# Reordering the opening of the input projection in a hybrid-decoder kernel on one Trainium2 core

## The chip, the cores and the metric

The kernel runs on one core of one Trainium2 chip. The metric is the device time of one execution in microseconds (us); the median of three runs is compared. Five engines are named as in the profile: PE (TensorE: matmuls and transposes; PEld is its weight load), ACT (ScalarE), DVE (VectorE), POOL (GpSimd) and SP (SyncE, which here only issues transfers). Each runs its own list of instructions in order and waits for the others by semaphores. PE and PEld read SBUF and write PSUM, whose eight banks hold 128 x 512 floats each.

## The reference, cut to what matters

One decoder layer over 2048 tokens of 1024 channels. Only its first step is touched:

```python
z = rms_norm(h, norm_attn_g[i]) @ w_in[i]     # (2048, 1024) @ (1024, 2304)
# rms_norm: x * rsqrt(mean(x*x) + 1e-6) * g
```

The columns of z are queries, keys and values of eight attention heads, the inputs of a spatial gate, and 256 channels of a state-space layer. Attention adds a bias to its scores, looked up from rel_bias (32 buckets x 8 heads) by distance; the kernel makes all the bias lines it needs once, inside the same stage.

## The kernel before

The whole kernel is a sequence of stages (input projection, attention, state space, mixing, feed-forward, final part). Each stage ends with a barrier over all engines. The change is in the first stage, `project_in`, which takes the time from 0 to about 460 us.

**Tiling.** The tokens go in G = 4 groups of 512 (four tiles of 128 rows, TILES = 4), the columns of `w_in` in NBLK = 9 blocks of 256, the 1024 input channels in KC = 8 chunks of 128. Each operand is split into a high part and the remainder, and each product is three matmuls per chunk (high by high, high by low, low by high), accumulated over the eight chunks. The order is written out by hand: for each group, all nine column blocks.

**What happens for a group before its products.** ACT squares the four row tiles with a running sum (`square`, L1044); DVE adds epsilon (L1102); ACT takes the root (`root`, L1049); DVE inverts it (L1104) and multiplies each of the four row tiles by it in place (`scale_rows`, L1107). PE transposes the scaled rows, one chunk of channels (four 128 x 128 transposes) a time, into one PSUM bank (`turn`, L1139). ACT writes the high part of that bank to SBUF, scaled by the gain (`split_x`, L1053), DVE the remainder (its own `split_x`, L1111). The turns alternate between two banks (`turn_bank`), so turn k waits until the remainder of turn k - 2 is written.

**Weights.** SP loads a block of weights (`load_w`, L970, 1 MB); ACT writes its high part (`split_w`, L1059), POOL the remainder (L1186). Two weight buffers alternate, so the load of block B + 2 waits for POOL's remainder of block B.

**PSUM.** Four banks (`product_bank`) take the products in turn, two (`turn_bank`) the transposes, two (`spare_bank`) are spare. The three matmuls of the bias look-up (L1165, one for each attention branch, 33 x 8 by 33 x 384) use the two spare banks and the last product bank; DVE copies them out (L1121).

**Order at the start.** SP issues four row tiles (L966), weight block 0, the look-up table (L1007), after a wait for a DVE memset the bias rows (L1009), weight block 1, seven small parameter loads, and then waits for the three bias copies before it goes on to the main loop. ACT: four squares, `split_w(0)`, `root(0)`, eight `split_x`, then the main loop, which begins with `split_w(1)`. DVE: memset, `scale_rows(0)`, eight `split_x`, three bias copies, a spreading copy of a parameter (L755), then group 1. PE: eight turns, the look-up, a wait for all eight remainders and for the three bias copies, and then the products of the main loop, each block behind its `w_lo_ready`. The lines of PE's opening:

```python
for k in range(KC):
    turn(0, k)
pe.wait_ge(bias_loaded, 2 * DMA)
for b in range(NB):
    pe.matmul(bias_bank[b][0:NH, 0:BAND], per_head[:, :], lookup[:, b, :], start=True, stop=True).then_inc(looked_up, 1)
pe.wait_ge(lo_written, KC)
pe.wait_ge(bias_copied, NB)
```

Of the kernel before, what the change touches and what calls it, by code (L numbers as in the profile page):

```python
# [22 lines left out]
P = 128  # L23
# [285 lines left out]
BAND = 384  # L309
# [571 lines left out]
def project_in(nc, x, gain, w_in, qk_hi, qk_lo, z, u_channels, rel_bias, bias_table, bias_lines, bands, bands_stored, parameters, head_ahead, ident):  # L881
# [27 lines left out]
    with Stage(nc, "in") as st:  # L909
# [30 lines left out]
        block = st.block()  # L940
        parameters.allocate(st, spare_bank[0], rows.rearrange("p t d -> p (t d)"), squares[:, 0, 0:2 * P], spare[:, 0:2 * P])
        assert nc.sbuf_base <= SSM_AT, nc.sbuf_base
        bias_bank = [spare_bank[0], spare_bank[1], product_bank[RING - 1]]

        def blocks():
            for g in range(G):
# [16 lines left out]
        def _(sp):  # L963
# [39 lines left out]
                    sp.dma_start(dst, src).then_inc(head_ahead.loaded, DMA)  # L1003

            load_x(0)
            load_w(0)
            sp.dma_start(lookup[:, :, :], bias_table).then_inc(bias_loaded, DMA)  # L1007
            sp.wait_ge(ones_set, 1)
            sp.dma_start(per_head[0:BUCKETS, :], rel_bias).then_inc(bias_loaded, DMA)  # L1009
            load_w(1)  # L1010
            parameters.load(sp)
            sp.wait_ge(bias_copied, NB)
# [24 lines left out]
        @block.scalar  # L1037
        def _(act):
            def square(g, t):
                n = g * TILES + t  # L1040
                act.wait_ge(x_loaded[t], (g + 1) * DMA)
                if n >= 2:
                    act.wait_ge(mean_ready, n - 1)
                nc.scalar.activation(squares[:, n % 2], rows[:, t], ACT.Square, scale=D ** -0.5,  # L1044
                                     accum_out=mean_sq[:, g, t:t + 1]).then_inc(mean_ready, 1)

            def root(g):
                act.wait_ge(eps_added, g + 1)
                nc.scalar.activation(rms[:, g], mean_sq[:, g], ACT.Sqrt).then_inc(rms_ready, 1)  # L1049

            def split_x(g, k):
                act.wait_ge(transposed, g * KC + k + 1)
                nc.scalar.activation(hi[:, g % 2, k, :], turn_bank[k % 2][:, :], ACT.Identity, scale=g_cols[:, k:k + 1]).then_inc(hi_written, 1)  # L1053

            def split_w(B):
                act.wait_ge(w_loaded[B % 2], (B // 2 + 1) * DMA)
                if B >= 2:
                    act.wait_ge(product_ready, units_to[B - 1])
                nc.scalar.copy(w_hi[B % 2][:, :, :], w_raw[B % 2][:, :, :]).then_inc(w_hi_ready, 1)  # L1059

            def evict(u):
                r = u % RING
                width = BANK if is_qk[u] else WIDE
                if u >= RING:
                    act.wait_ge(stored[r], stores_through(u - RING))
                act.wait_ge(product_ready, u + 1)
                if is_qk[u]:
                    nc.scalar.copy(result_hi[:, r, :], product_bank[r][:, :]).then_inc(result_hi_ready, 1)
                if is_u[u]:
                    nc.scalar.copy(result[:, r, :].rearrange("p (l m) -> p l m", l=L),  # L1070
                                   product_bank[r].rearrange("p (m l) -> p l m", l=L)).then_inc(copied, 1)
                else:
                    nc.scalar.copy(result[:, r, 0:width], product_bank[r][:, 0:width]).then_inc(copied, 1)

            for t in range(TILES):
                square(0, t)
            split_w(0)
            root(0)
            act.wait_ge(gain_loaded, DMA)
            for k in range(KC):  # L1080
                split_x(0, k)
            for g, b, B in blocks():
                if B + 1 < G * NBLK:
                    split_w(B + 1)
                if g + 1 < G:
                    if 1 <= b <= TILES:
                        square(g + 1, b - 1)
                    if b == TILES:
                        root(g + 1)
                    if b > LOOK:  # L1090
                        for k in (2 * (b - LOOK - 1), 2 * (b - LOOK - 1) + 1):
                            split_x(g + 1, k)
                if B == (G - 1) * NBLK + LOOK + 1:
                    parameters.root(act)
                for u in units_of(B):
                    evict(u)

        @block.vector
        def _(dve):
            def scale_rows(g):  # L1100
                dve.wait_ge(mean_ready, (g + 1) * TILES)
                nc.vector.tensor_scalar(mean_sq[:, g], mean_sq[:, g], EPS, None, ALU.add).then_inc(eps_added, 1)  # L1102
                dve.wait_ge(rms_ready, g + 1)
                nc.vector.reciprocal(rstd[:, g], rms[:, g]).then_inc(rstd_ready, 1)  # L1104
                dve.wait_ge(rstd_ready, g + 1)
                for t in range(TILES):
                    nc.vector.tensor_scalar(rows[:, t], rows[:, t], rstd[:, g, t:t + 1], None, ALU.mult).then_inc(rows_scaled, 1)  # L1107

            def split_x(g, k):
                dve.wait_ge(hi_written, g * KC + k + 1)  # L1110
                nc.vector.scalar_tensor_tensor(lo[:, g % 2, k, :], turn_bank[k % 2][:, :], g_cols[:, k:k + 1],  # L1111
                                               hi[:, g % 2, k, :].bitcast(F32), ALU.mult, ALU.subtract).then_inc(lo_written, 1)

            nc.vector.memset(per_head[:, :], 1.0).then_inc(ones_set, 1)
            scale_rows(0)
            dve.wait_ge(gain_loaded, DMA)
            for k in range(KC):
                split_x(0, k)
            for b in range(NB):
                dve.wait_ge(looked_up, b + 1)  # L1120
                nc.vector.tensor_copy(bias_rows[:, b, :], bias_bank[b][0:NH, 0:BAND]).then_inc(bias_copied, 1)  # L1121
            parameters.spread_dt(dve)
            for g in range(1, G):
                scale_rows(g)
# [8 lines left out]
        def _(pe):  # L1133
            def turn(g, k):
                pe.wait_ge(rows_scaled, (g + 1) * TILES)
                if g * KC + k >= 2:
                    pe.wait_ge(lo_written, g * KC + k - 1)
                for t in range(TILES):
                    mm = pe.transpose(turn_bank[k % 2][:, t * P:(t + 1) * P], rows[:, t, k * P:(k + 1) * P], ident[:, :])  # L1139
                mm.then_inc(transposed, 1)  # L1140

            def product(u, g, B, n):
# [5 lines left out]
                        pe.wait_ge(result_hi_ready, qk_to[u - RING] + 1)  # L1148
                part = slice(n * P, (n + 1) * P)
                for k in range(KC):  # L1150
                    if is_qk[u] or is_u[u]:
                        pe.matmul(out[:, :], w_hi[w][:, k, part], x_hi[:, k, :], start=(k == 0), stop=False)
                        pe.matmul(out[:, :], w_hi[w][:, k, part], x_lo[:, k, :], start=False, stop=False)
# [4 lines left out]
                        mm = pe.matmul(out[:, 0:WIDE], x_lo[:, k, part], w_hi[w][:, k, :], start=False, stop=(k == KC - 1))  # L1158
                mm.then_inc(product_ready, 1)

            for k in range(KC):
                turn(0, k)
            pe.wait_ge(bias_loaded, 2 * DMA)
            for b in range(NB):
                pe.matmul(bias_bank[b][0:NH, 0:BAND], per_head[:, :], lookup[:, b, :], start=True, stop=True).then_inc(looked_up, 1)  # L1165
            pe.wait_ge(lo_written, KC)
            pe.wait_ge(bias_copied, NB)
            for g, b, B in blocks():
                if b == 0:
                    pe.wait_ge(lo_written, (g + 1) * KC)  # L1170
                if g + 1 < G and b > LOOK:
                    for k in (2 * (b - LOOK - 1), 2 * (b - LOOK - 1) + 1):
# [2116 lines left out]
```

## Time and profile before

| | us |
|---|---|
| runs, median (lowest to highest of three) | 2695.56 (2693.56 to 2697.71) |
| the profiled execution, its own time | 2699.88 |
| span of its trace | 2698.3 |
| mean granted clock of PE over the span | 0.975 |
| PE busy over the span | 2529.6 |

The span runs from the first to the last instruction of the trace; the execution's own time holds 1.58 us more around it. All times in the views are counted from the start of the span. The duration of a matmul in the trace is modelled at its end, and successive matmuls overlap, so a row that merges several gives start and total length, and their pace is read from the distance of starts.

### The profile page before, as it was taken

The page shows a single profiled execution, that of the slowest core. Times are in us where ns is not written, and L with a number is a line of the kernel's source. Part 1 is how long each engine was busy: PE and PEld are TensorE (multiplying, and loading weights), DVE is VectorE, ACT ScalarE, POOL GpSimd, SP SyncE. Part 2 cuts the span into 40 slices and gives each one's busy share as a digit, 9 for nine tenths or more (in the row PEclk, how much of TensorE's full clock was granted, in tenths as well). Part 3 has the DMA queues.
Part 4 walks back from the last instruction along what each step waited for, and adds up shares of the span by engine and source line. Part 5 has one row for each costly group of instructions (what it writes and reads, how often), then busy time and mean ns, then how long its engine had stood idle before and what let it go on. Part 6 is the DMA issues. An engine that isn't in the chain of part 4 may idle for free. (4 is left out here: it accounts for less than half of the span.)

```text
span 2698.3 us, 38124 instructions
## 1 busy us (share of the span) xinstructions
PE 2529.6 (94%) x13395; PEld 2169.2 (80%) x13395; DVE 1805.3 (67%) x3343; ACT 1347.5 (50%) x2425; POOL 825.7 (31%) x625
## 2 busy tenths in 40 slices
PE   6999999999976899699999989999999999999998
PEld 4989888999965688588888868888888877887876
DVE  2113276777766777689999976768898885563433
ACT  3343432666644666555555545545555554344544
POOL 2554544656620221235565540001222221000000
PEclk9999999999987899899999999999999999999999
DMA  4675564788853355134444477543232336763211
GB/s 160 200 221 172 164 178 144 179 180 186 174 154 122 105 168 200 56 122 148 163 154 157 153 270 265 188 164 99 100 114 98 106 133 222 285 224 110 81 70 49
DMA packets 317450, 420.97 MB, mean 156 GB/s; under 512 B 31073, under 2 KB 229025, under 8 KB 312522
## 3 DMA queue, kind: packets, MB, share of 16 engines
q1 hardware_dynamic: 292090, 332.68, 40.9%
q0 software_dynamic: 25184, 86.01, 8.6%
q8 instruction: 102, 1.67, 0.3%
q14 instruction: 74, 0.61, 0.1%
HBM read 298.59 MB, written 124.16 MB: 157 GB/s over the span
## 5 line engine op out<-in xcount | busy, mean ns | idle before, releaser
L2783 PE MATMUL ffn_bank<-ffn_x,ffn_ring 128*128 128x512 f32 x704 | 275.9, 392 | 15.3 <-DVE ffn_strips L2583 9.2
L2784 PE MATMUL ffn_bank<-ffn_x,ffn_ring 128*128 128x512 f32 x704 | 274.8, 390 | 0.0
L2785 PE MATMUL ffn_bank<-ffn_x,ffn_ring 128*128 128x512 f32 x704 | 274.7, 390 | 0.0
L2851 POOL DMA_DIRECT2D ffn_act<-ffn_late x154 | 85.6, 557 | 474.5 <-DVE ffn_late L2615 444.4
L1186 POOL TENSOR_TENSOR in_w_lo<-in_w,in_w_hi 128x2048 fp32r<-128x2048 f32 x36 | 168.1, 4670 | 191.2 <-ACT in_w_hi L1059 191.2
L2783 PE MATMUL ffn_bank<-tail_shared,ffn_ring 128*128 128x512 f32 x528 | 206.7, 392 | 9.3 <-DVE ffn_ring L2558 7.8
L629 ACT ACTIVATE att_exps<-att_scores,att_part 128x256 f32<-128x256 f32 (+1 forms) x384 | 152.9, 454 | 107.4 <-DVE att_part L597 104.9
L2785 PE MATMUL ffn_bank<-tail_shared,ffn_ring 128*128 128x512 f32 x528 | 206.4, 391 | 0.0
L2380 ACT COPY ffn_strips<-ffn_bank 128x512 f32<-128x512 f32 x176 | 103.5, 588 | 144.1 <-PE ffn_bank L2785 144.1
L2599 DVE SCALAR_TENSOR_TENSOR ffn_strips<-ffn_strips,ffn_taps 128x512 f32<-128x512 f32 x176 | 143.9, 818 | 41.1 <-ACT ffn_strips L2395 41.1
L2783 PEld LDWEIGHTS ffn_bank<-ffn_x,ffn_ring 128*128 128x128 f32 x704 | 132.6, 188 | 46.0 <-issue 11.5
L567 PE MATMUL att_bank<-att_v,att_expsT 128*128 128x66 f32 x1200 | 154.2, 270 | 5.3 <-DMA att_v<-z_rows 4.0
L2566 DVE TENSOR_TENSOR ffn_ring<-ffn_w,ffn_ring 128x2048 fp32r<-128x2048 f32 (+1 forms) x42 | 91.1, 2169 | 98.2 <-ACT ffn_ring L2354 98.2
L2785 PEld LDWEIGHTS ffn_bank<-ffn_x,ffn_ring 128*128 128x128 f32 x704 | 132.7, 188 | 28.0
L2784 PEld LDWEIGHTS ffn_bank<-ffn_x,ffn_ring 128*128 128x128 f32 x704 | 132.7, 189 | 27.3
L567 PEld LDWEIGHTS att_bank<-att_v,att_expsT 128*128 128x128 f32 x1200 | 147.7, 193 | 7.0 <-issue 4.2
L2602 DVE SCALAR_TENSOR_TENSOR ffn_strips<-ffn_strips,ffn_taps 128x512 f32<-128x512 f32 x176 | 141.8, 806 | 6.2
L1156 PE MATMUL in_bank<-in_w_hi,in_hi 128*128 128x256 f32 x512 | 145.8, 285 | 0.0
L1157 PE MATMUL in_bank<-in_w_lo,in_hi 128*128 128x256 f32 x512 | 144.8, 283 | 0.0
L1158 PE MATMUL in_bank<-in_w_hi,in_lo 128*128 128x256 f32 x512 | 144.8, 283 | 0.0
L2345 ACT CAST ffn_ring<-ffn_sums 128x512 fp32r<-128x512 f32 x176 | 107.9, 614 | 62.7 <-PE ffn_bank L2785 52.2
L2784 PE MATMUL ffn_bank<-ffn_x_lo,ffn_ring 128*128 128x512 f32 x352 | 137.0, 389 | 0.0
(437 smaller groups left out, 7375.8 us busy)
## 6 DMA issues: line engine op xcount, KB each, us to landing
ffn_w<-in_ffn_w_up SPq DMA_DIRECT2D x88, 512.0 KB, 4.8
ffn_act<-ffn_late POOLq DMA_DIRECT2D x154, 256.0 KB, 2.3
in_w<-in_w_in SPq DMA_DIRECT2D x36, 1024.0 KB, 6.5
ffn_a_raw<-ffn_act SPq DMA_DIRECT2D x77, 256.0 KB, 3.7
ffn_a_raw_later<-ffn_act SPq DMA_DIRECT2D x77, 256.0 KB, 4.5
ffn_w<-ffn_down_sums SPq DMA_DIRECT2D x16, 1024.0 KB, 5.2
ffn_w<-in_ffn_w_down SPq DMA_DIRECT2D x12, 1024.0 KB, 5.7
ffn_pieces<-in_ffn_w_down POOLq DMA_DIRECT2D x44, 256.0 KB, 3.5
```

The costliest lines, as they stand in the source:

```text
L567: mm = pe.matmul(out, expsT[:, n % 2, piece * P:(piece + 1) * P], vals[:, b, blk, h * ROW:(h + 1) * ROW], start=(at == 0), stop=(at == len ...
L629: nc.scalar.activation(exps[:, n % RING, m * width:(m + 1) * width], scores[:, n % RING, m * width:(m + 1) * width], ACT.Exp, bias=part[:, ...
L1156: pe.matmul(out[:, 0:WIDE], x_hi[:, k, part], w_hi[w][:, k, :], start=(k == 0), stop=False)
L1157: pe.matmul(out[:, 0:WIDE], x_hi[:, k, part], w_lo[w][:, k, :], start=False, stop=False)
L1158: mm = pe.matmul(out[:, 0:WIDE], x_lo[:, k, part], w_hi[w][:, k, :], start=False, stop=(k == KC - 1))
L1186: nc.gpsimd.tensor_tensor(w_lo[B % 2][:, :, :], w_raw[B % 2][:, :, :], w_hi[B % 2][:, :, :].bitcast(F32), ALU.subtract).then_inc(w_lo_read ...
L2345: nc.scalar.copy(slot(j)[0], src).then_inc(w_hi_ready, 1)
L2599: nc.vector.scalar_tensor_tensor(conv[:, n, tg], raw[f % 2][:, n, 1 + tg * BANK:1 + (tg + 1) * BANK], tap[1], conv[:, n, tg], ALU.mult, AL ...
L2602: nc.vector.scalar_tensor_tensor(conv[:, n, tg], raw[f % 2][:, n, tg * BANK:(tg + 1) * BANK], tap[0], conv[:, n, tg], ALU.mult, ALU.add).t ...
L2783: pe.matmul(out[:, :], hi[:, k], x_hi[kind][:, k], start=(k == 0 and fresh), stop=False, skip_group_check=not fresh)
L2784: pe.matmul(out[:, :], hi[:, k], x_lo[kind][:, k], start=False, stop=False, skip_group_check=not fresh)
L2785: mm = pe.matmul(out[:, :], lo[:, k], x_hi[kind][:, k], start=False, stop=(k == KH - 1), skip_group_check=not fresh)
```

## The change

It is confined to the opening of `project_in`, group 0. PE does the bias look-up first and the eight turns after it. The eight turns of group 0 go to eight different banks (`first_turns`: product banks 0 to 2, the two turn banks, then the three banks of the look-up, whose order is changed so that the last product bank comes first), so none waits for a remainder any more; the last three wait for the bias copies of their bank. PE's wait for all eight remainders before the first products is replaced by one wait for each chunk inside the first product (unit u = 0). ACT takes the root ahead of `split_w(0)`, and scales two of the four row tiles of group 0 itself (a new function, `scale_first_rows`); DVE scales the other two, and makes the bias copies ahead of its eight remainders. SP issues the look-up table and the bias rows ahead of weight block 0. Groups 1 to 3 and everything after are as before.

```diff
@@ -940,7 +940,9 @@
         block = st.block()
         parameters.allocate(st, spare_bank[0], rows.rearrange("p t d -> p (t d)"), squares[:, 0, 0:2 * P], spare[:, 0:2 * P])
         assert nc.sbuf_base <= SSM_AT, nc.sbuf_base
-        bias_bank = [spare_bank[0], spare_bank[1], product_bank[RING - 1]]
+        bias_bank = [product_bank[RING - 1], spare_bank[0], spare_bank[1]]
+        first_turns = product_bank[0:RING - 1] + turn_bank + bias_bank
+        SCALED_BY_DVE = TILES // 2
 
         def blocks():
             for g in range(G):
@@ -1003,10 +1005,10 @@
                     sp.dma_start(dst, src).then_inc(head_ahead.loaded, DMA)
 
             load_x(0)
-            load_w(0)
             sp.dma_start(lookup[:, :, :], bias_table).then_inc(bias_loaded, DMA)
             sp.wait_ge(ones_set, 1)
             sp.dma_start(per_head[0:BUCKETS, :], rel_bias).then_inc(bias_loaded, DMA)
+            load_w(0)
             load_w(1)
             parameters.load(sp)
             sp.wait_ge(bias_copied, NB)
@@ -1048,9 +1050,15 @@
                 act.wait_ge(eps_added, g + 1)
                 nc.scalar.activation(rms[:, g], mean_sq[:, g], ACT.Sqrt).then_inc(rms_ready, 1)
 
+            def scale_first_rows():
+                act.wait_ge(rstd_ready, 1)
+                for t in range(SCALED_BY_DVE, TILES):
+                    nc.scalar.activation(rows[:, t], rows[:, t], ACT.Copy, scale=rstd[:, 0, t:t + 1]).then_inc(rows_scaled, 1)
+
             def split_x(g, k):
                 act.wait_ge(transposed, g * KC + k + 1)
-                nc.scalar.activation(hi[:, g % 2, k, :], turn_bank[k % 2][:, :], ACT.Identity, scale=g_cols[:, k:k + 1]).then_inc(hi_written, 1)
+                src = turn_bank[k % 2] if g else first_turns[k]
+                nc.scalar.activation(hi[:, g % 2, k, :], src[:, :], ACT.Identity, scale=g_cols[:, k:k + 1]).then_inc(hi_written, 1)
 
             def split_w(B):
                 act.wait_ge(w_loaded[B % 2], (B // 2 + 1) * DMA)
@@ -1074,8 +1082,9 @@
 
             for t in range(TILES):
                 square(0, t)
+            root(0)
+            scale_first_rows()
             split_w(0)
-            root(0)
             act.wait_ge(gain_loaded, DMA)
             for k in range(KC):
                 split_x(0, k)
@@ -1103,22 +1112,23 @@
                 dve.wait_ge(rms_ready, g + 1)
                 nc.vector.reciprocal(rstd[:, g], rms[:, g]).then_inc(rstd_ready, 1)
                 dve.wait_ge(rstd_ready, g + 1)
-                for t in range(TILES):
+                for t in range(TILES if g else SCALED_BY_DVE):
                     nc.vector.tensor_scalar(rows[:, t], rows[:, t], rstd[:, g, t:t + 1], None, ALU.mult).then_inc(rows_scaled, 1)
 
             def split_x(g, k):
                 dve.wait_ge(hi_written, g * KC + k + 1)
-                nc.vector.scalar_tensor_tensor(lo[:, g % 2, k, :], turn_bank[k % 2][:, :], g_cols[:, k:k + 1],
+                src = turn_bank[k % 2] if g else first_turns[k]
+                nc.vector.scalar_tensor_tensor(lo[:, g % 2, k, :], src[:, :], g_cols[:, k:k + 1],
                                                hi[:, g % 2, k, :].bitcast(F32), ALU.mult, ALU.subtract).then_inc(lo_written, 1)
 
             nc.vector.memset(per_head[:, :], 1.0).then_inc(ones_set, 1)
             scale_rows(0)
+            for b in range(NB):
+                dve.wait_ge(looked_up, b + 1)
+                nc.vector.tensor_copy(bias_rows[:, b, :], bias_bank[b][0:NH, 0:BAND]).then_inc(bias_copied, 1)
             dve.wait_ge(gain_loaded, DMA)
             for k in range(KC):
                 split_x(0, k)
-            for b in range(NB):
-                dve.wait_ge(looked_up, b + 1)
-                nc.vector.tensor_copy(bias_rows[:, b, :], bias_bank[b][0:NH, 0:BAND]).then_inc(bias_copied, 1)
             parameters.spread_dt(dve)
             for g in range(1, G):
                 scale_rows(g)
@@ -1133,10 +1143,13 @@
         def _(pe):
             def turn(g, k):
                 pe.wait_ge(rows_scaled, (g + 1) * TILES)
-                if g * KC + k >= 2:
+                if g:
                     pe.wait_ge(lo_written, g * KC + k - 1)
+                elif first_turns[k] in bias_bank:
+                    pe.wait_ge(bias_copied, bias_bank.index(first_turns[k]) + 1)
+                out = turn_bank[k % 2] if g else first_turns[k]
                 for t in range(TILES):
-                    mm = pe.transpose(turn_bank[k % 2][:, t * P:(t + 1) * P], rows[:, t, k * P:(k + 1) * P], ident[:, :])
+                    mm = pe.transpose(out[:, t * P:(t + 1) * P], rows[:, t, k * P:(k + 1) * P], ident[:, :])
                 mm.then_inc(transposed, 1)
 
             def product(u, g, B, n):
@@ -1148,6 +1161,8 @@
                         pe.wait_ge(result_hi_ready, qk_to[u - RING] + 1)
                 part = slice(n * P, (n + 1) * P)
                 for k in range(KC):
+                    if u == 0:
+                        pe.wait_ge(lo_written, k + 1)
                     if is_qk[u] or is_u[u]:
                         pe.matmul(out[:, :], w_hi[w][:, k, part], x_hi[:, k, :], start=(k == 0), stop=False)
                         pe.matmul(out[:, :], w_hi[w][:, k, part], x_lo[:, k, :], start=False, stop=False)
@@ -1158,15 +1173,13 @@
                         mm = pe.matmul(out[:, 0:WIDE], x_lo[:, k, part], w_hi[w][:, k, :], start=False, stop=(k == KC - 1))
                 mm.then_inc(product_ready, 1)
 
-            for k in range(KC):
-                turn(0, k)
             pe.wait_ge(bias_loaded, 2 * DMA)
             for b in range(NB):
                 pe.matmul(bias_bank[b][0:NH, 0:BAND], per_head[:, :], lookup[:, b, :], start=True, stop=True).then_inc(looked_up, 1)
-            pe.wait_ge(lo_written, KC)
-            pe.wait_ge(bias_copied, NB)
+            for k in range(KC):
+                turn(0, k)
             for g, b, B in blocks():
-                if b == 0:
+                if b == 0 and g:
                     pe.wait_ge(lo_written, (g + 1) * KC)
                 if g + 1 < G and b > LOOK:
                     for k in (2 * (b - LOOK - 1), 2 * (b - LOOK - 1) + 1):
```

## Rows read from the trace of the kernel before

**Rows 1.** Page: span, and busy time of each engine.

```profile
span 2698.3 us, 38124 instructions
...
PE 2529.6 (94%) x13395; PEld 2169.2 (80%) x13395; DVE 1805.3 (67%) x3343; ACT 1347.5 (50%) x2425; POOL 825.7 (31%) x625
```

**Rows 2.** Windows: stretch and length, then busy time and count of each engine, clock, DMA.

```profile
0.00:38.40 38.40, 11.72 (x38) 6.62 (x38) 13.31 (x19) 16.55 (x21) 8.21 (x9) 1.00 0.37 117
38.40:100.00 61.60, 60.14 (x266) 49.78 (x267) 10.23 (x7) 21.69 (x32) 31.71 (x13) 1.00 0.65 210
```

**Rows 3.** Waits of PE, whole span: who waited for whom, total, times, longest.

```profile
PE in_bank L1139 <- DVE in_rows L1107: 27.2, 4, 23.5
...
PE in_bank L1152 <- POOL in_w_lo L1186: 4.4, 1, 4.4
```

**Rows 4.** Timeline, 0 to 23.5 us: start, length, engine, line, operation, idle before.

```profile
2.56 1.28 ACT L1044 ACT_TABLE_LOAD   x1 [2.56 <-PEq L139]
...
6.21 1.06 ACT L1044 ACTIVATE in_squares<-in_rows 128x1024 f32<-128x1024 f32 x1 [2.37 <-DMA in_rows<-in_x]
...
12.13 0.19 ACT L1044 ACTIVATION_READ_ACCUMULATOR in_squares<-in_rows 128x1 f32 x1
...
14.44 1.90 ACT L1059 CAST in_w_hi<-in_w 128x2048 fp32r<-128x2048 f32 x1 [2.13 <-DMA in_w<-in_w_in]
16.36 1.28 ACT L1049 ACT_TABLE_LOAD   x1
16.42 4.49 POOL L1186 TENSOR_TENSOR in_w_lo<-in_w,in_w_hi 128x2048 fp32r<-128x2048 f32 x1 [12.24 <-ACT in_w_hi L1059]
17.65 0.21 ACT L1049 ACTIVATE in_rms<-in_mean_sq 128x4 f32<-128x4 f32 x1
...
18.10 5.35 DVE L1107 TENSOR_SCALAR in_rows<-in_rows,in_rstd 128x1024 f32<-128x1024 f32 x4
```

**Rows 5.** Line L1107 over the span: shortest, median and longest duration in ns.

```profile
L1107 DVE TENSOR_SCALAR in_rows<-in_rows,in_rstd x16: 740/748/3364, 18.1 to 307.4; 128x1024 f32<-128x1024 f32 x16
```

**Rows 6.** Transfers in two stretches: 0 to 10 us, and 12.5 to 14.5 us.

```profile
DMA packets 593, 2.05 MB, mean 205 GB/s; under 512 B 85, under 2 KB 96, under 8 KB 593
...
DMA packets 551, 0.61 MB, mean 303 GB/s; under 512 B 75, under 2 KB 518, under 8 KB 551
```

**Rows 7.** Timeline, 23.5 to 38.8 us, from the first turn to the first products.

```profile
23.51 1.97 PE L1139 MATMUL in_bank<-whole_ident,in_rows 128*128 128x128 f32 x8 [23.51 <-DVE in_rows L1107]
24.72 1.48 ACT L1053 ACTIVATE in_hi<-in_bank,in_gain 128x512 fp32r<-128x512 f32 x2 [6.86 <-PE in_bank L1139]
...
31.01 1.60 DVE L1111 SCALAR_TENSOR_TENSOR in_lo<-in_bank,in_gain,in_hi 128x512 fp32r<-128x512 f32 x2 [1.14 <-ACT in_hi L1053]
...
31.91 1.94 PE L1139 MATMUL in_bank<-whole_ident,in_rows 128*128 128x128 f32 x8 [0.80 <-DVE in_lo L1111]
...
33.78 4.00 PE L1165 MATMUL in_bank<-in_lookup,in_per_head 33*8 33x384 f32 x6
...
37.82 0.55 DVE L1121 COPY in_bias_rows<-in_bank 8x384 f32<-8x384 f32 x1 [0.73 <-PE in_bank L1165]
...
38.47 0.76 PE L1152 MATMUL in_bank<-in_hi,in_w_hi 128*128 128x512 f32 x1 [0.69 <-issue]
...
38.74 0.40 SPq L970 DMA_DIRECT2D in_w<-in_w_in  x1
```

**Rows 8.** Windows around the first products, columns as in rows 2.

```profile
38.45:43.30 4.85, 4.83 (x12) 3.79 (x13) 2.59 (x1) 0.00 (x0) 2.51 (x1) 1.00 0.72 220
43.30:52.10 8.80, 8.80 (x40) 7.27 (x39) 0.00 (x0) 0.65 (x2) 0.00 (x0) 1.00 0.75 272
```

**Rows 9.** Line L1139 at groups 1 to 3: durations in ns.

```profile
L1139 PE MATMUL in_bank<-whole_ident,in_rows x88: 272/273/331, 109.4 to 346.1; 128*128 128x128 f32 x88
```

**Rows 10.** Waits of ACT, 40 to 460 us, columns as in rows 3.

```profile
ACT in_w_hi L1059 <- DMA in_w<-in_w_in: 29.9, 11, 6.6
```

**Rows 11.** Windows of two later stretches, columns as in rows 2.

```profile
870.00:900.00 30.00, 18.07 (x72) 14.54 (x72) 24.58 (x48) 21.31 (x32) 6.54 (x6) 0.73 0.10 37
...
960.00:990.00 30.00, 30.00 (x152) 25.33 (x152) 23.60 (x59) 20.01 (x40) 5.92 (x9) 1.00 0.56 169
```

## The prediction, made before the changed kernel ran

> **What bounds the kernel now.** I read the page first. PE is busy 94% of the span [rows 1], so a change can gain only where PE stands still, or where it works slower than it could. The windows then say where that is at the start: in the first 38.4 us PE works 11.7 us, and from there to 100 us it works 60.1 of 61.6 us [rows 2]. The waits of PE say what the standstill is made of: one wait of 23.5 us for the scaled rows of group 0, the longest single wait of PE that this change touches [rows 3]. So the opening is a chain of latencies that ends when the first product starts at 38.47 [rows 7]; after it PE runs almost without a gap. What the change is worth is how much earlier that product starts, less what comes back later.
>
> The timeline gives the chain. The four squares end at 12.32. ACT then goes into the weight split, which waits for its weights until 14.44 and takes 1.90; only then come the table load of 1.28, the root at 17.65, and the scaling by DVE from 18.10 to 23.45 [rows 4]. Those four scalings last 5.35 together, although the median of one is 0.748; one of the sixteen in the kernel lasted 3.364 [rows 5]. It is the first: POOL's remainder of the weights runs from 16.42 to 20.91 [rows 4], and three of 0.66 each before 23.45 put its end at 21.46, just after POOL's. So 2.7 us of the scaling is DVE held while POOL works. Then the turns: two banks let PE do two, then it waits; the first pair starts at 23.51 and the fourth at 31.91, 2.80 a pair, of which 1.87 is PE's work (31.91 to 33.78). The look-up takes 4.0, its last copy ends at 38.37, and the product follows [rows 7].
>
> **The change part by part.** Times are on the clock of this trace.
>
> *Root ahead of the weight split.* The table load follows the last square at 12.33. A load need not stand behind what its activation waits for: the first one ran at 2.56, 3.65 us ahead of the square that waited for its rows [rows 4]. Load 12.33 to 13.62; root to 13.83; from the root's start to the first scaling the trace has 0.45 (17.65 to 18.10), so scaling starts at 14.08 instead of 18.10.
>
> *Scaling by two engines.* DVE: two tiles, 0.66 and 0.75, end 15.5, with POOL idle until then, since its work comes behind the weight split that ACT now does later. ACT: the form with a factor for each row is not in the trace at this size; the nearest row is the square of the same tile, 1.06 [rows 4]. Two give 2.1, so ACT ends at 16.2. Below it cannot be under 1.9 (the cast of 2048 columns, 1.90); above, 2.3: by 1.06 for 1024 columns and 1.90 for 2048, 512 would take 0.64, and the evacuation of 512 with a factor takes 0.74 [rows 7], so a factor may add 0.1 to each tile. Rows are ready at 16.2 instead of 23.5.
>
> *Look-up first.* It costs PE 4.0 at the head of its queue, behind the landing of the two bias transfers; behind it stand all turns. The rows of x are 2.1 MB, and 2.05 MB had moved by 10.0 [rows 6]; the table (148.5 KB) now follows them directly, so I take 11.9 for its landing. The fourth row tile was being squared by 11.1 to 11.2 (1.06 a square, its sum read at 12.13 [rows 4]), and nothing behind it lands earlier; the transfers of under 512 B between 12.5 and 14.5, 75 of them [rows 6], hold the tail of both weight block 0 and the bias rows, so 14.5 is the other end. Look-up 11.9 to 15.9: hidden under the scaling, with 0.3 to spare. Landing at 14.5 would put the first turn at 18.5 and so cost 2.3. The three copies on DVE (0.55 each) run from 15.9 to 17.6; turn 5, the first that needs one, comes at about 20.7.
>
> *Weight block 0 behind the table.* SP issues it later, but its packets wait behind x anyway. It lands later by the time of 148.5 KB, about 0.5 us at the pace of the first 10 us, at 15.0 instead of 14.44. ACT comes to it at 16.2: hidden.
>
> *ACT and POOL.* Weight split 16.2 to 18.1; POOL's remainder starts 0.06 to 0.08 later and takes 4.5 [rows 4]: ready at 22.7. Then ACT writes eight high parts at 0.74 each, 18.1 to 24.0. DVE's remainders at 0.80 each (1.60 for two) follow to 25.3 [rows 7].
>
> *Eight banks.* The turns run without a stop. Four pairs at 1.87 are 7.5; that counts the handover to another kind of matmul four times instead of once, so I take 7.2 (6.1 would be the least, if the 0.42 by which the last transpose overhangs a pair is taken off each). Turns 16.2 to 23.4.
>
> *Wait for each chunk.* The first product needs the remainder of chunk 0 (19.6), POOL's 22.7, and PE free at 23.4. Chunk k is ready at 19.6 + 0.8k and wanted at 23.4 + 1.2k (twelve matmuls, four chunks, took 4.85 [rows 8]). No wait. First product: 23.4, set by PE's turns, with POOL 0.7 behind.
>
> *Behind it.* Block 1 is wanted 13.6 us after the first product (38.47 to about 52.1), at 37.0. ACT splits its weights 24.0 to 25.9, POOL is done at 30.5. SP's next loads wait for POOL (22.7) and the last turn (23.4): weight block 2, issued at 38.74, or 0.27 after the first product [rows 7], goes out about 0.7 before it. The spreading copy on DVE comes at 25.3. None is late. Each later stage starts behind a barrier, so it only moves.
>
> **Sum.** 38.47 less 23.4 is 15.1 us. The profiled execution, 2699.88, would become 2684.8; it stood 4.3 above the median of its runs, 2695.56, so the median becomes 2680.5, or 0.56% less. About 0.2% (5.4 us) is what a measurement of this kernel can tell from no change.
>
> **The rivals.**
>
> *The clock rises before the products.* The first twelve matmuls took 0.40 each, the next forty 0.22 [rows 8]: the first stretch is 1.2 GHz by its pace, the second 2.4, although the granted clock reads 1.00 in both. Now PE would have 11.5 us of work without a real gap before the product, where it had stops of 0.9 in each pair. If the clock rose in there, a transpose would last 273 ns [rows 9] for the 0.42 here, the turns would end by 21, POOL (22.7) would start the products, and the twelve would take 2.7 instead of 4.85. That is 15.8 + 2.1 = 17.9, or 2677.7. Against it: in the old order PE worked from 31.91 to 37.8 without a stop, transposes and look-up, and the twelve were still slow. The Trainium skill ("TensorE: Matmul & The Clock Gate", section "Part 4: PE-mode transpose") says that transposes do not count as PE being busy for the clock; by it this rival falls, and the opening here agrees as far as it goes.
>
> *The bias lands late.* PE stands before the look-up until 14.5: 18.5 + 7.2 = 25.7, a gain of 12.8, or 2682.8. For it: the small transfers in the window to 14.5. Against: these lay behind a megabyte of weights that is no longer in front.
>
> *No change: the gain is given back in the stream of weights.* ACT waited eleven times for weights, 29.9 in all [rows 10], and PE 4.4 once for what follows from it [rows 3]. If loads were bound to something that doesn't move, PE would meet them earlier; 9.7 us of new standstill would bring the time within 0.2% (2690 to 2695.6). Against: every load waits for a POOL or PE step that moves too.
>
> *Slower: a later stretch falls to the lower clock.* At 870 to 900 us the granted clock was 0.73, with PE busy 18.1 of 30; at 960 to 990 it was 1.00, with PE busy throughout [rows 11]. Work of PE done anew at half the clock costs its own length again, so from 20.5 us of such work on the kernel is slower by over 0.2% (above 2701). Against: the clock follows PE's own pauses there, which come from chains that only move in time.
>
> **How the numbers follow.** Chances: my forecast 0.74, clock early 0.12, bias late 0.08, gain given back 0.04, slower 0.02. So faster 0.94, same 0.04, slower 0.02. The time is that of the forecast, 2680.5. The range takes in the two cases next to it (2677.7 and 2682.8) and the spread of a median of runs that differ by 2 us to either side (2693.56 to 2697.71 before), with one more for the bounds of ACT's scaling and the turns: 2675 to 2687.
>
> **What would show it.** In the new profile: table load at 12.3, root at 13.6, first scaling at 14.1 with no DVE scaling over 0.8 us; look-up from 11.9 to 15.9; 32 transposes in one run from 16.2 to 23.4; POOL's first remainder ready at 22.7; first product at 23.4, its first twelve matmuls at 0.40; standstill of PE from 38.4 on no larger than before. The forecast is wrong if the table load waits, if ACT's scaling takes over 1.3 a tile, if the look-up starts after 12.5, or if PE's waits behind 40 us grow by more than 5.

## The result, and the profile after

The changed kernel takes 2677.57 us (median of four runs, 2675.45 to 2681.47) against 2695.72 for the kernel before beside it: ratio 0.9939, 95% interval 0.9926 to 0.9951, or 18.2 us less. The forecast was 15.1 less (2680.5), the range 2675 to 2687. Run once more beside other kernels it gave 2680.45 against 2698.45, ratio 0.9930 (0.9915 to 0.9944). The gain is real and larger than forecast by about 3 us; it is very near the rival to which the prediction gave 0.12, that PE's clock rises before the products (2677.7).

The page and the windows of the changed kernel, answering to [rows 1, 2, 8]; the third window has the length of the first of [rows 8] (in a window: length, then busy time and count of PE, PEld, DVE, ACT and POOL, PE's granted clock, busy share of the DMA engines, GB/s):

```profile
span 2677.4 us, 38120 instructions
...
PE 2528.1 (94%) x13395; PEld 2169.1 (81%) x13395; DVE 1797.1 (67%) x3341; ACT 1349.0 (50%) x2427; POOL 824.7 (31%) x625
...
0.00:23.08 23.08, 10.17 (x38) 6.56 (x38) 7.07 (x14) 15.62 (x21) 6.32 (x8) 1.00 0.65 196
23.08:84.68 61.60, 60.16 (x286) 50.44 (x287) 9.82 (x11) 26.74 (x37) 34.70 (x14) 1.00 0.68 221
...
23.08:27.93 4.85, 4.83 (x21) 4.03 (x22) 1.82 (x4) 2.55 (x3) 2.22 (x1) 1.00 0.77 243
```

The stretch before the first product is 15.3 us shorter, with the same instructions of PE in it (38, by [rows 2] too). The 61.6 us behind it hold 286 matmuls where they held 266, with the same busy time: PE does not only start earlier, it works faster at the start. The 4.85 us that held 12 matmuls hold 21.

The timeline of the opening, answering to [rows 4, 7] (the three matmuls of the look-up stand as six in the trace):

```profile
12.46 4.00 PE L1178 MATMUL in_bank<-in_lookup,in_per_head 33*8 33x384 f32 x6 [12.46 <-DMA in_per_head<-in_rel_bias]
12.47 0.19 ACT L1046 ACTIVATION_READ_ACCUMULATOR in_squares<-in_rows 128x1 f32 x1
...
12.67 1.28 ACT L1051 ACT_TABLE_LOAD   x1
...
13.97 0.21 ACT L1051 ACTIVATE in_rms<-in_mean_sq 128x4 f32<-128x4 f32 x1
...
14.42 2.19 ACT L1056 ACTIVATE in_rows<-in_rows,in_rstd 128x1024 f32<-128x1024 f32 x2 [0.25 <-DVE in_rstd L1113]
14.42 1.42 DVE L1116 TENSOR_SCALAR in_rows<-in_rows,in_rstd 128x1024 f32<-128x1024 f32 x2
...
16.52 1.88 ACT L1067 CAST in_w_hi<-in_w 128x2048 fp32r<-128x2048 f32 x1
16.66 6.17 PE L1152 MATMUL in_bank<-whole_ident,in_rows 128*128 128x128 f32 x32 [0.20 <-ACT in_rows L1056]
...
18.48 4.56 POOL L1199 TENSOR_TENSOR in_w_lo<-in_w,in_w_hi 128x2048 fp32r<-128x2048 f32 x1 [14.30 <-ACT in_w_hi L1067]
19.10 5.68 DVE L1121 SCALAR_TENSOR_TENSOR in_lo<-in_bank,in_gain,in_hi 128x512 fp32r<-128x512 f32 x8 [1.88 <-ACT in_hi L1061]
...
23.10 0.50 PE L1167 MATMUL in_bank<-in_hi,in_w_hi 128*128 128x512 f32 x1 [0.27 <-POOL in_w_lo L1199]
23.43 0.40 PE L1168 MATMUL in_bank<-in_lo,in_w_hi 128*128 128x512 f32 x1
23.67 0.39 PE L1169 MATMUL in_bank<-in_hi,in_w_lo 128*128 128x512 f32 x1
```

The table load stands right behind the last square, both engines scale at once, the 32 transposes go in one run, and the first product waits 0.27 for POOL. The second and third product are 0.24 apart, where the first twelve of the old opening are 0.43 apart: the clock is up already. The durations of the transposes show where it rose (line L1152 in 20.5 to 21, 21.5 to 22 and 22 to 23 us; shortest, median, longest in ns), to be held against the 273 ns of [rows 9]:

```profile
L1152 PE MATMUL in_bank<-whole_ident,in_rows x5: 421/421/421, 20.1 to 21.0; 128*128 128x128 f32 x5
...
L1152 PE MATMUL in_bank<-whole_ident,in_rows x5: 272/334/421, 21.2 to 21.9; 128*128 128x128 f32 x5
...
L1152 PE MATMUL in_bank<-whole_ident,in_rows x8: 272/272/273, 21.8 to 22.6; 128*128 128x128 f32 x8
```

So it rose between 21.4 and 21.8, inside the turns: the first transpose at the short duration starts 5.1 us behind the first of them. PE's waits, answering to [rows 3]:

```profile
PE in_bank L1178 <- DMA in_per_head<-in_rel_bias: 12.5, 1, 12.5
...
PE in_bank L1167 <- POOL in_w_lo L1199: 4.7, 2, 4.5
PE in_bank L1152 <- DVE in_rows L1116: 3.7, 3, 1.4
```

The 23.5 us of standstill are 12.5. What was left over for groups 1 to 3 (3.7) and for the weights (4.4, now 4.7 with the 0.27 above) is as before. By the line views the last products of the stage begin at 447.8 instead of 465.8 and attention at 450.0 instead of 468.0: 18.0 us, of which 15.4 are the earlier first product and 2.3 the faster first dozen (the thirteenth matmul starts at 25.95 instead of 43.64); the remaining 0.3 comes behind the long wait for weights, which ends 17.7 earlier (388.22 and 405.92).

### The profile page after: what moved, and what is told of

It is laid out like the page before. It is cut to its first block and busy times, and to the rows that moved or that the text cites. A ratio compares the mean times of both kernels' runs of the same rounds, so it can differ in the third digit from the quotient of the medians.

```text
span 2677.4 us, 38120 instructions
## 1 busy us (share of the span) xinstructions
PE 2528.1 (94%) x13395; PEld 2169.1 (81%) x13395; DVE 1797.1 (67%) x3341; ACT 1349.0 (50%) x2427; POOL 824.7 (31%) x625
```

## The experiments

Theory A: a run of transposes without a stop raises PE's clock; the old opening had the same transposes with a stop in every pair. Rivals: B, it is PE's whole work from the look-up on; C, transposes count for nothing and the look-up did it. The other experiments price the parts. Since the landing of x varies from run to run (the last square's sum was read between 11.7 and 12.6), starts of the first product are also given from the ready rows.

**Root alone, in the old order** (`root_alone`).

```diff
-            split_w(0)
             root(0)
+            split_w(0)
             act.wait_ge(gain_loaded, DMA)
```

> The kernel before with one line moved: the root ahead of the weight split. If the chain of the prediction holds, DVE starts scaling at about 14.1, its fourth tile starts at 16.1, ahead of POOL's remainder at 16.4, so the rows are ready at 16.8 instead of 23.5 and the first product starts at 31.8 instead of 38.5: 6.7 us gained, ratio 0.9975. Rival: DVE's last tile comes a little late, POOL is first and holds it until about 21: rows ready at 21.5, 2 us gained, ratio 0.9993. In both the first twelve products stay at 0.40 each, since the turns stop after each pair as before.

Measured: 2691.65 against 2697.24, ratio 0.9981 (0.9971 to 0.9990). The timeline:

```profile
13.68 2.74 DVE L1107 TENSOR_SCALAR in_rows<-in_rows,in_rstd 128x1024 f32<-128x1024 f32 x4
...
16.14 4.67 POOL L1186 TENSOR_TENSOR in_w_lo<-in_w,in_w_hi 128x2048 fp32r<-128x2048 f32 x1 [11.97 <-ACT in_w_hi L1059]
16.48 1.97 PE L1139 MATMUL in_bank<-whole_ident,in_rows 128*128 128x128 f32 x8 [16.48 <-DVE in_rows L1107]
...
31.44 0.77 PE L1152 MATMUL in_bank<-in_hi,in_w_hi 128*128 128x512 f32 x1 [0.68 <-issue]
```

Four tiles take 2.74 on DVE instead of 5.35, as the last of them has begun before POOL starts, and the first product starts 7.0 us earlier (31.44 against 38.47). One moved line gives 7.0 of the 15.4 in the trace; the medians differ by 5.6. The first nine products are slow (0.43 apart), where it was twelve.

**Look-up behind the turns** (`lookup_behind`): the turns have nothing ahead of them.

```diff
-            pe.wait_ge(bias_loaded, 2 * DMA)
-            for b in range(NB):
-                pe.matmul(bias_bank[b][0:NH, 0:BAND], per_head[:, :], lookup[:, b, :], start=True, stop=True).then_inc(looked_up, 1)
             for k in range(KC):
                 turn(0, k)
+            pe.wait_ge(lo_written, KC)
+            pe.wait_ge(bias_loaded, 2 * DMA)
+            for b in range(NB):
+                pe.matmul(bias_bank[b][0:NH, 0:BAND], per_head[:, :], lookup[:, b, :], start=True, stop=True).then_inc(looked_up, 1)
```

(DVE's copies go behind its remainders, and the wait for them to the product that reuses the bank; the waits inside the first product go.)

> The changed kernel with the look-up behind the eight turns (and behind all remainders) instead of ahead of them. Theory A: a run of transposes without a stop raises PE's clock by itself. Then the pace of the turns rises about 4.9 us behind the first turn, near 21.5, as in the changed kernel (16.66 and 21.5). Theory B: it is PE's whole run from the look-up on, or the look-up itself, that raised it. Then all 32 transposes stay at 421 ns. In both, PE stands from the last turn to the last remainder (about 2 us), the look-up costs 2 to 4 us in front of the products, so the first product starts at 27 to 29.5: 4 to 8 us slower than the changed kernel, ratio to before 0.9955 to 0.997.

Measured: 2683.38, ratio 0.9953 (0.9940 to 0.9967). PE's timeline, and two windows:

```profile
16.50 5.51 PE L1150 MATMUL in_bank<-whole_ident,in_rows 128*128 128x128 f32 x32 [16.50 <-ACT in_rows L1056]
...
24.38 2.10 PE L1179 MATMUL in_bank<-in_lookup,in_per_head 33*8 33x384 f32 x6 [2.36 <-DVE in_lo L1121]
...
27.30:30.60 3.30, 3.30 (x9) 2.59 (x8) 2.39 (x1) 0.00 (x0) 2.31 (x1) 0.52 0.66 164
30.60:33.00 2.40, 2.40 (x12) 1.97 (x11) 0.00 (x0) 0.00 (x0) 0.00 (x0) 1.00 1.08 396
```

The transposes alone raise the clock: 32 in 5.51, the first at the short duration 3.8 us behind the first of all (4.9 was expected), and the look-up then takes 2.10 instead of 4.00. B and C fall. The first product starts at 26.41, ahead of the expected 27 to 29.5. And the clock came down again, at 27, behind a stop of 2.36 and the look-up, with a granted clock of 0.52 until 30.6. So the look-up did not keep the clock up.

**Turns in two banks** (`two_banks`): the same turns with stops.

```diff
-        first_turns = product_bank[0:RING - 1] + turn_bank + bias_bank
+        first_turns = turn_bank * (KC // 2)
...
-                elif first_turns[k] in bias_bank:
-                    pe.wait_ge(bias_copied, bias_bank.index(first_turns[k]) + 1)
+                elif k >= 2:
+                    pe.wait_ge(lo_written, k - 1)
```

(The wait for the bias copies goes to the product that reuses their bank.)

> The changed kernel with the first eight turns in the two turn banks, each waiting for the remainder two turns back; all else as changed. The four pairs then take 2.8 us each: first turn at 16.6, first product at 27.0 instead of 23.1. Theory A (only turns without a stop raise the clock): no rise in the turns, the first twelve products at 0.40 each, so 3.9 + 2.1 = 6 us less gain, about 12 of 18, ratio 0.9955. Theory B (PE's work from the look-up on, stops or none): the rise comes at about 21.5 all the same, and the products start fast: 3.9 us less gain, ratio 0.9947.

Measured: 2685.31, ratio 0.9960 (0.9947 to 0.9974). The first product starts 10.4 us behind the first turn (26.40 and 15.99) instead of 6.4 (23.10 and 16.66). PE's timeline from the last pair of turns to the first products:

```profile
24.81 1.94 PE L1152 MATMUL in_bank<-whole_ident,in_rows 128*128 128x128 f32 x8 [0.80 <-DVE in_lo L1121]
26.40 0.78 PE L1169 MATMUL in_bank<-in_hi,in_w_hi 128*128 128x512 f32 x1
...
26.98 0.63 PE L1170 MATMUL in_bank<-in_lo,in_w_hi 128*128 128x512 f32 x1
...
27.40 0.56 PE L1171 MATMUL in_bank<-in_hi,in_w_lo 128*128 128x512 f32 x1
...
27.80 0.40 PE L1169 MATMUL in_bank<-in_hi,in_w_hi 128*128 128x512 f32 x1
```

The transposes with stops between them did not raise the clock in 10 us. The products were slow at first, as A has it, but three of them, not twelve. The last pair of turns runs into them without a stop, so here a stretch of work without a stop begins at 24.81, and the first fast product starts 3.0 us behind that. In the old opening and in `root_alone`, where a stop of 0.7 stands ahead of the products, the first fast one starts 5.2 and 3.9 behind the first product.

**Extra transposes ahead** (`turns_ahead`).

```diff
+            for n in range(44):
+                pe.transpose(product_bank[0][:, n % TILES * P:(n % TILES + 1) * P], ident[:, :], ident[:, :])
             pe.wait_ge(bias_loaded, 2 * DMA)
```

> The changed kernel with 44 extra transposes of the identity at the head of PE's queue, into a bank that the first turn overwrites; nothing reads them. Theory A: the clock rises inside them, 4 to 6 us behind their start near 3 us, the look-up takes about 2 us instead of 4.0, and the 32 turns come at full clock (273 ns, 4.3 us instead of 6.2). The first product then waits for POOL alone, at 23.0: time as for the changed kernel, within 0.5 us. Theory C (transposes do not count for the clock): the extra ones last 421 ns to their end, the look-up 4.0, and the turns rise no earlier than about 21.5.

Measured: 2680.44, ratio 0.9942 (0.9928 to 0.9955). PE's timeline:

```profile
2.60 6.31 PE L1177 MATMUL in_bank<-whole_ident 128*128 128x128 f32 x44 [2.60 <-PEq L139]
12.49 4.01 PE L1180 MATMUL in_bank<-in_lookup,in_per_head 33*8 33x384 f32 x6 [3.57 <-DMA in_per_head<-in_rel_bias]
16.77 6.43 PE L1152 MATMUL in_bank<-whole_ident,in_rows 128*128 128x128 f32 x32 [0.27 <-ACT in_rows L1056]
```

Half right. The clock rose inside the extra transposes: at the slow pace, 0.21 apart, 44 would take about 9.6 us (an estimate), and they took 6.3. But I had overlooked the stop until the bias landed: behind 3.57 us of it the look-up was slow (4.01) and the turns began slow again. The first product started at 23.20, near the expected 23.0, but not by the way expected.

**Prices of the other parts**, each undone by itself.

`weights_ahead`:

```diff
             load_x(0)
+            load_w(0)
             sp.dma_start(lookup[:, :, :], bias_table).then_inc(bias_loaded, DMA)
...
-            load_w(0)
             load_w(1)
```

> The changed kernel with weight block 0 issued ahead of the look-up table and the bias rows again. By the chain (look-up at PE's head, turns behind it) the bias lands between 13.5 and 14.5 instead of 12.46, the look-up ends at 17.5 to 18.5 instead of 16.46, and turns and first product come 1 to 2 us later (first product 24 to 25 instead of 23.1). Rival: the landing of the bias is set by what lies ahead of both, and it stays at 12.5: no difference.

`all_remainders`:

```diff
-                        pe.wait_ge(lo_written, k + 1)
+                        pe.wait_ge(lo_written, KC)
```

> The changed kernel with the first product waiting for all eight remainders instead of one for each chunk. The last remainder ended at 24.8 in the changed kernel, so the first product starts at 24.8 to 24.9 instead of 23.1: 1.7 us later. PE stands 2 us between turns and products. If the clock that the turns raised outlasts that stop, the products go at 0.23 each from the start; if not, the first ten or so take 0.43 and the loss is 1.7 + 2 = 3.7.

`root_behind`:

```diff
+            split_w(0)
             root(0)
             scale_first_rows()
-            split_w(0)
```

> The changed kernel with root and scaling behind the weight split again. Weights land at about 15, split to 16.9, table load and root to 18.4, scaling from 18.7. Theory: POOL's remainder (17.0 to 21.5) holds DVE's first tile until it ends, so a tile of DVE lasts over 3 us while ACT's two are done at 20.9; rows ready at 22.8, first turn 22.9, first product at 29.2, 6.1 later. Rival: POOL does not hold DVE, both engines scale at once: rows ready at 20.9, first product at 27.2, 4.1 later.

`scaled_by_dve`:

```diff
-        SCALED_BY_DVE = TILES // 2
+        SCALED_BY_DVE = TILES
```

> The changed kernel with all four tiles of group 0 scaled by DVE. DVE takes 14.4 to 17.2, ACT splits the weights from their landing at 15 on, POOL starts at 17.0, behind the start of DVE's last tile (16.4). Rows ready at 17.2 instead of 16.6, first product 0.4 to 0.6 later, and POOL 1.5 earlier than before it is needed. Rival: POOL comes ahead of DVE's last tile and holds it until 21.5, first product 5 later.

Measured, beside 2700.03 for the kernel before: 2683.18, ratio 0.9937 (0.9919 to 0.9954); 2684.20, 0.9944 (0.9927 to 0.9961); 2689.41, 0.9959 (0.9945 to 0.9973); 2678.34, 0.9924 (0.9908 to 0.9941). By their times only the third stands apart from the changed kernel (0.9930, 0.9915 to 0.9944), and barely: its interval overlaps that of the changed kernel's first measurement (0.9926 to 0.9951). All four are read from the timelines. `weights_ahead`, then `all_remainders`:

```profile
15.59 4.00 PE L1178 MATMUL in_bank<-in_lookup,in_per_head 33*8 33x384 f32 x6 [15.59 <-DMA in_per_head<-in_rel_bias]
...
24.84 0.48 PE L1167 MATMUL in_bank<-in_hi,in_w_hi 128*128 128x512 f32 x1
```

```profile
24.40 0.47 PE L1167 MATMUL in_bank<-in_hi,in_w_hi 128*128 128x512 f32 x1 [2.51 <-DVE in_lo L1121]
24.71 0.40 PE L1168 MATMUL in_bank<-in_lo,in_w_hi 128*128 128x512 f32 x1
```

Behind 1 MB of weights the bias lands at 15.59, not at 14.5 as I had bounded it, and the first product is 1.7 later than in the changed kernel. Waiting for all remainders costs 1.3 (1.5 from the table load, which stood 0.23 earlier here), and the clock outlasts a stop of 2.51: the second product follows 0.31 behind the first. `root_behind`, then `scaled_by_dve`:

```profile
16.95 4.51 POOL L1199 TENSOR_TENSOR in_w_lo<-in_w,in_w_hi 128x2048 fp32r<-128x2048 f32 x1 [12.78 <-ACT in_w_hi L1067]
...
18.63 2.19 ACT L1056 ACTIVATE in_rows<-in_rows,in_rstd 128x1024 f32<-128x1024 f32 x2 [0.24 <-DVE in_rstd L1113]
18.64 4.04 DVE L1116 TENSOR_SCALAR in_rows<-in_rows,in_rstd 128x1024 f32<-128x1024 f32 x2
...
28.93 0.48 PE L1167 MATMUL in_bank<-in_hi,in_w_hi 128*128 128x512 f32 x1
```

```profile
14.36 2.74 DVE L1116 TENSOR_SCALAR in_rows<-in_rows,in_rstd 128x1024 f32<-128x1024 f32 x4
...
17.16 6.37 PE L1152 MATMUL in_bank<-whole_ident,in_rows 128*128 128x128 f32 x32 [1.00 <-DVE in_rows L1116]
...
23.29 0.49 PE L1167 MATMUL in_bank<-in_hi,in_w_hi 128*128 128x512 f32 x1
```

POOL holds DVE: two tiles take 4.04 beside POOL's remainder and 1.42 without it, while ACT's two take 2.19 in both. Not all of DVE's work is held: in the changed kernel its eight remainders, which read a PSUM bank, take 5.68 beside POOL's work from 18.48 to 23.04, 0.71 each. The order of root and split is worth 5.8 here. The second engine is worth 0.2: its rows are ready 0.5 earlier, but POOL's work then starts 1.6 later (18.48 against 16.89) and is what the product waits for.

**A version with more cover** (`filled`), beside the changed kernel again (`changed_again`). Three tiles on DVE and one on ACT, so that POOL starts earlier, and extra transposes in PE's idle time, so that the clock is up before the turns.

```diff
-        SCALED_BY_DVE = TILES // 2
+        SCALED_BY_DVE = TILES - 1
...
+            fill(76)
             pe.wait_ge(bias_loaded, 2 * DMA)
             for b in range(NB):
                 pe.matmul(bias_bank[b][0:NH, 0:BAND], per_head[:, :], lookup[:, b, :], start=True, stop=True).then_inc(looked_up, 1)
+            fill(16)
             for k in range(KC):
                 turn(0, k)
```

(`fill(n)` issues n transposes of the identity into the bank of the first turn.)

> The changed kernel with three tiles of group 0 scaled by DVE and one by ACT, and with extra transposes of the identity on PE in its idle time: 76 ahead of the look-up and 16 between look-up and turns, into a bank that the first turn overwrites. Theory A (transposes raise the clock, a stop or the look-up lets it fall): the clock is up when the look-up starts at 12.4, so it takes about 2.1 instead of 4.0, and the 32 turns take 3.8 instead of 6.2 if the fill carries the clock across; they end before 21. POOL, free to start 1.1 us earlier, is ready at 22.0, and the first product starts there, 1.1 us before the changed kernel's 23.1. Rival: the clock falls in the look-up all the same, the turns take 6.2 and end at 22.8: 0.3 us gained. The time itself moves by too little to be told apart.

> The changed kernel once more, beside the filled one and the kernel before on the same chip: first product at 23.0 to 23.2 if the landing of x varies as it did (last square read at 12.0 to 12.6), and a ratio near 0.9935; the median of the filled one within 3 us of it.

Measured: 2679.58, ratio 0.9928 (0.9915 to 0.9942), and for the changed kernel 2680.45, ratio 0.9930 (0.9915 to 0.9944). PE's timeline of the filled kernel, with its one long wait late in the stage; below it the same wait of the changed kernel:

```profile
12.34 2.10 PE L1183 MATMUL in_bank<-in_lookup,in_per_head 33*8 33x384 f32 x6
...
16.40 3.71 PE L1152 MATMUL in_bank<-whole_ident,in_rows 128*128 128x128 f32 x32
...
21.91 0.50 PE L1167 MATMUL in_bank<-in_hi,in_w_hi 128*128 128x512 f32 x1 [1.80 <-POOL in_w_lo L1205]
...
388.51 0.80 PE L1167 MATMUL in_bank<-in_hi,in_w_hi 128*128 128x512 f32 x1 [5.83 <-POOL in_w_lo L1205]
```

```profile
388.48 0.80 PE L1167 MATMUL in_bank<-in_hi,in_w_hi 128*128 128x512 f32 x1 [4.57 <-POOL in_w_lo L1199]
```

The opening does what A says: look-up 2.10, 32 turns in 3.71, first product 1.3 earlier (21.91; 23.21 in the changed kernel here, where the table load stood 0.27 later). In this execution nothing of it is left at 388.5, as PE waits 5.83 for a late block of weights instead of 4.57. That the earlier opening caused the longer wait is not shown: the wait is 5.8 in `two_banks`, `weights_ahead` and `turns_ahead` too, whose first products start at 26.40, 24.84 and 23.20, no earlier than the changed kernel's 23.10. The line of `turns_ahead`, with its first product at 23.20:

```profile
389.71 0.79 PE L1167 MATMUL in_bank<-in_hi,in_w_hi 128*128 128x512 f32 x1 [5.83 <-POOL in_w_lo L1201]
```

In `filled` and `turns_ahead` alike ACT waits 8.45 for this block's load instead of 7.74, and POOL's remainder takes 5.06 instead of 4.50. The version is not told apart from the changed kernel by its time.

## Why the prediction came out as it did

**Root ahead: right.** Scaling was forecast for 14.08 and came at 14.42; 0.34 of that is the last square, ended at 12.66 instead of 12.32. The table load waits for nothing: it starts 0.01 behind the square. That POOL held DVE for 2.7 us, and that the new order frees DVE, is shown by `root_behind` (4.04 for two tiles) and `root_alone` (2.74 for four). The copy L755, which lasted 2.74 beside POOL's work in the old order, lasts 0.20.

**Two engines: right in time, idle in effect.** ACT takes 2.19 for two tiles, inside 1.9 to 2.3. What I did not see is that the second engine holds the weight split back, and with it POOL by 1.6, so that POOL becomes what the first product waits for; undone, it costs 0.2.

**Look-up first, table ahead of the weights: right.** Landing 12.46, inside 11.2 to 14.5 (11.9 taken); PE had 0.20 to spare. That is at the edge of 12.5 which the prediction named as a sign of being wrong (12.52 in `changed_again`); it stayed hidden because the rows came 0.4 late too. The rival of a late landing did not come. My upper end came from the old order, and with that order the bias landed at 15.59 (`weights_ahead`): a bound that was too low, without effect. The 0.5 us taken for 148.5 KB at the pace of the first 10 us should be 0.74 at the 205 GB/s of [rows 6]; ACT did not wait for these weights, so nothing hung on it.

**Eight banks and the wait for each chunk: right, sizes close.** Turns to the first product took 6.4 instead of 7.2, partly by the clock: at the slow pace, 31 steps of 0.213 from 16.66 would put the start of the last transpose at 23.3 (an estimate), beside the 23.4 of the sum. POOL was ready at 23.04 against 22.7 and thus last, 0.27 behind PE. No wait for a remainder shows in the first product.

**The clock: the step that failed.** The sum let the first twelve products stay slow, and gave the early rise 0.12. It came: 21 matmuls in 4.85 us, worth 2.3 by the thirteenth product. I had read from the old opening that 5.9 us of work without a stop, transposes and look-up, left the twelve slow. But four of these were look-up, and the look-up did not count with them: the changed kernel has 4.0 of it right ahead of the turns, and its first short transpose comes 5.1 us behind the first turn, against 3.8 in `lookup_behind`, which has none there. The transposes raise the clock by themselves once they run without stops. The rule of the Trainium skill on which I leaned ("TensorE: Matmul & The Clock Gate", section "Part 4: PE-mode transpose": transposes do not count as busy) differs from what is measured here, for transposes of 128 x 128 floats: 421 ns each, then 272 from 21.8 on.

**Behind the opening: right.** PE's long wait for late weights stayed at 4.45, and the stage ends 18.0 earlier. Behind the stage single profiled executions drift further (the changed kernel's last matmul begins 20.8 earlier, `scaled_by_dve` gains 15.8 in the stage and 23.3 at the end); the medians of the changed kernel and the kernel before differ by 18.2, the stage's share. The rival of the weight stream was wrong for this change. Whether it holds for an opening that is earlier still is open: the longer wait of `filled` also stands in three kernels whose opening is no earlier.

**Open.** The number of slow products (twelve, nine and three in three openings with stops) goes with how far the rise comes behind the start of a stretch without a stop. In ten runs of transposes without a stop the first short one starts 2.8 to 5.7 us behind the first; what sets this distance was not settled, nor how short a stop must be for the clock to rise all the same.

## What to carry to other kernels

At the start of a kernel, look for the short step that every other one needs and move it ahead of any long one that waits for a transfer; here one moved line brought the first product 7 us forward. See which engine holds another while it works, and put the held work ahead of it. Where PE has to start from the low clock, transposes in one run, with a bank for each group of them, save twice: the stops between them, and the products at the low clock behind them (4.0 us to the first product in `two_banks`, and three products at the low clock).

## What the runs showed of the hardware that was not expected

- Transposes issued without a stop bring PE from 1.2 to 2.4 GHz: the first at the short duration starts 5.1 us behind the first of all in the changed kernel, 2.8 in `turns_ahead`. With stops of 0.8 to 1.4 us between pairs they did not in 10 us.
- Four microseconds of the 33 x 8 by 33 x 384 look-up did not raise the clock: the transposes 0.2 us behind it started at 421 ns. A look-up of 2.1 us between two runs of transposes, at full clock, let it stay (`filled`: the 32 turns in 3.71).
- The clock outlasted a stop of 2.51 us followed by products, and came down behind a stop of 2.36 us followed by the look-up (one execution each).
- The windows give a granted clock of 1.00 for the slow products of the old opening [rows 8], and 0.52 for those of `lookup_behind`, where the clock had been up before: at the start of a trace the level is read from the distance of the matmuls, not from that column.
